# A pool map in plain fp32 from unsplit operands, and the order of the work around it, in a hybrid decoder step on one Trainium2 core

## What is computed

```python
h = modulate(rms_norm(x, g_pre_mix), shift_m, scale_m)
u, q, k, v, z_pool, z_att = jnp.split(h @ w_in, IN_SPLITS, axis=-1)
# branch A, 4 groups of 256 channels, windows 2, 4, 8, 16
pooled = window_mean(u_ext) - u
mixed  = jnp.einsum('btgc,gcd->btgd', pooled, w_map)          # the pool map
y_pool = (mixed * scale) @ w_proj_pool
# branch B: dilated window attention, 3 groups merged by their denominators
y_att  = o @ w_proj_att
mix = (sigmoid(z_pool) * y_pool + sigmoid(z_att) * y_att) @ w_out
x = x + gate_m * rms_norm(mix, g_post_mix)
# then up-projection, causal conv of 3, GeGLU, down-projection, norm
```

## Time and profile before

| | |
|---|---|
| runs, median | 1136.33, 1133.63, 1133.76; 1133.76 us |
| the profiled execution's own time | 1135.69 us |
| its span in the profile | 1133.8 us |
| mean granted TensorE clock | 0.955 |
| PE busy | 1059.3 us (93%), 8653 matmul records |
| DVE / ACT / POOL busy | 485.5 / 417.8 / 119.7 us |
| DMA | 216 MB, mean 191 GB/s |

### The profile page before, as it was taken

How to read it: one execution, slowest core, us unless ns; L and a number is a source line. 1 busy time by engine, 2 the same in 40 slices (tenths; PEclk the granted TensorE clock), 3 DMA queues, 4 the chain that set the end, 5 groups by cost and what they waited for, 6 DMA issues and landing times.

```text
span 1133.8 us, 20595 instructions
## 1 busy us (share of the span) xinstructions
PE 1059.3 (93%) x8653; PEld 991.8 (87%) x8653; DVE 485.5 (43%) x884; ACT 417.8 (37%) x667; POOL 119.7 (11%) x165
## 2 busy tenths in 40 slices
PE   5999999999999999979898795599999999999996
PEld 3899999999999999868748794599999999999994
DVE  5533233322432244254814335656565655522224
ACT  5424423332443234244202233544444544422222
POOL 1000300040004001405402202200000000000000
PEclk8899999999999999979999897699999999999996
DMA  9885767567656774243926537066666666555312
GB/s 324 247 277 199 224 223 250 186 216 244 236 186 212 244 243 131 77 139 120 309 98 199 184 111 252 27 198 225 223 224 222 219 220 210 156 172 162 117 36 75
DMA packets 226856, 216.01 MB, mean 191 GB/s; under 512 B 6173, under 2 KB 191901, under 8 KB 226749
## 3 DMA queue, kind: packets, MB, share of 16 engines
q1 hardware_dynamic: 226765, 214.70, 58.2%
HBM read 207.27 MB, written 96.03 MB: 268 GB/s over the span
## 4 chain that ended last, share of the span: by engine, by line
PE 87%; DVE 5%; ACT 2%; POOL 2%; issue 1%; SPq 1%; DMA 1%; ACTq 0%; POOLq 0%; DVEq 0%
PE acc L1289 74%; PE psT L1581 2%; PE psS L1453 2%; PE psT L1467 2%; PE psS L1333 2%; POOL tha L630 1%; POOL ssq L590 1%; PE psS L1441 1%; PE psS L1343 1%; DMA ada_first<-in_w_ada 1%; PE psT L1481 1%; PE psS L1439 1%; PE psS L1557 1%; DVE xT L1233 1%; ACT norm_u L680 1%
## 5 line engine op out<-in xcount | busy, mean ns | idle before, releaser
L1289 PE MATMUL acc<-act_hi,w_hi 128*128 128x260 f32 x1824 | 379.3, 289 | 20.4 <-DVE act_lo L1138 7.2
L1289 PE MATMUL acc<-act_hi,w_lo 128*128 128x260 f32 x1824 | 371.0, 285 | 0.0
L1289 PE MATMUL acc<-act_lo,w_hi 128*128 128x260 f32 x1824 | 370.7, 285 | 0.0
L892 DVE TENSOR_TENSOR w_lo<-raw,w_hi 128x1024 fp32r<-128x1024 f32 x150 | 191.7, 1279 | 374.7 <-ACT w_hi L651 374.1
L1289 PEld LDWEIGHTS acc<-act_hi,w_hi 128*128 128x128 f32 x1824 | 284.9, 191 | 29.3 <-issue 23.9
L1289 PEld LDWEIGHTS acc<-act_lo,w_hi 128*128 128x128 f32 x1824 | 285.3, 191 | 0.0
L1289 PEld LDWEIGHTS acc<-act_hi,w_lo 128*128 128x128 f32 x1824 | 284.9, 191 | 0.0
L651 ACT ACTIVATE w_hi<-raw 128x1024 fp32r<-128x1024 f32 x150 | 157.0, 1046 | 203.7 <-PE acc L1289 193.7
L1289 PE MATMUL acc<-g_hi,w_hi 128*128 128x260 f32 x352 | 71.0, 283 | 0.0
L1289 PE MATMUL acc<-g_hi,w_lo 128*128 128x260 f32 x352 | 70.8, 282 | 0.0
L1289 PE MATMUL acc<-g_lo,w_hi 128*128 128x260 f32 x352 | 70.6, 282 | 0.0
(11 more groups left out here) (248 smaller groups left out, 1126.9 us busy)
## 6 DMA issues: line engine op xcount, KB each, us to landing
out_k_sample<-in_cache_k_w SPq DMA_DIRECT2D x89, 368.0 KB
out_v_sample<-in_cache_v_w SPq DMA_DIRECT2D x89, 368.0 KB
raw<-in_w_in SPq DMA_DIRECT2D x60, 512.0 KB, 6.1
raw<-in_w_up SPq DMA_DIRECT2D x44, 512.0 KB, 5.8
ada_mid<-in_w_ada SPq DMA_DIRECT2D x11, 1024.0 KB, 9.8
ada_first<-in_w_ada SPq DMA_DIRECT2D x9, 1024.0 KB, 9.4
raw<-in_w_down SPq DMA_DIRECT2D x16, 512.0 KB, 4.1
out_k_sample<-in_cache_k_w SPq DMA_DIRECT2D x16, 511.0 KB
```

The costliest lines, as they stand in the source:

```text
L892: dve.tensor_tensor(w_lo[PLACE[n]][:, 0:cols], raw[:, n % RAW, 0:cols], w_hi[PLACE[n]][:, 0:cols].bitcast(F32), ALU.subtract).then_inc(lo_ ...
L1289: ins_ = pe.matmul(acc[b][:, half, 0:HALF], w, x[:, t, half * HALF:(half + 1) * HALF], start=first and i == 0 and j == 0, stop=last and i ...
```

## The change

The map's sums are made by plain fp32 matmuls straight from `uT` and from `raw` (`map_unit`): two blocks, two halves, no split of either. The map's two units are left out of `PLACE`/`SPLITS`, so the splits that ran for them two units ahead now run for pp0 and pp1. `pooled_hi` and the VectorE half of it go. PE's order is now: map unit 0, then the second fold, move_stat and the transposes, then map unit 1, then spread_shares, then pp0. ScalarE and VectorE follow the same order; `join` comes behind the last sum of the map. The cast rounds move from `MID` places 1 to 6 to places 2 to 7 (round 0 with pp0, round 5 with pp5), the transposes of `u_tail` from the end of the map to the end of pp1. `mixed_hi/lo` are now the memory of `act_hi/lo`, and four of the six places of cached keys and values move to the memory of `qkvT` and `uT`.

```diff
-PLACE = [0, 1, 2] + [n % 2 for n in range(1, len(UNITS) - 2)]
+PLACE = {0: 0, 1: 1, 2: 2}
+for n in range(3, len(UNITS)):
+    if UNITS[n][0] != "map":
+        PLACE[n] = 1 - PLACE[max(m for m in PLACE if PLACE[m] < 2)]
+SPLITS = sorted(PLACE)
+SPLIT = {n: i for i, n in enumerate(SPLITS)}
...
         @block.sync
-                if n >= RAW:
-                    sp.wait_ge(lo_ready, n - RAW + 1)
+                if n >= RAW and n - RAW in SPLIT:
+                    sp.wait_ge(lo_ready, SPLIT[n - RAW] + 1)
+                elif n >= RAW:
+                    sp.wait_ge(unit_done, n - RAW + 1)
...
         @block.scalar
-                            split(N[s] + 2)
+                            split(SPLITS[N[s] + 2])
...
-            weights(PAIRS - 1)
-            pooled_hi(0)
-            pooled_hi(1)
-
-            act.wait_ge(rows_turned, 1)
...
             for pos, (what, m) in enumerate(MID):
-                if 1 <= pos < 7:
-                    i = pos - 1
+                if pos == 1:
+                    weights(PAIRS - 1)
+                    act.wait_ge(rows_turned, 1)
+                    act.activation(qhl[0:64, :], psS[0:64, 0:DA], ACT.Copy)
...
+                if pos == 2:
+                    joined(PAIRS - 1)
+                    act.wait_ge(o_lod, PAIRS)
...
+                if 2 <= pos < 8:
+                    i = pos - 2
...
         @block.tensor
+            def map_unit(m):
+                n = N["map", m, 0]
+                pe.wait_ge(raw_full[n % RAW], 16 * (n // RAW + 1))
+                for q in range(4):
+                    i, g, d = 4 * m + q, 2 * m + q // 2, q % 2
+                    pe.wait_ge(pooled, g + 1)
+                    take(("map", i))
+                    for kt in range(2):
+                        w = blk(raw[:, n % RAW, :], 4 * (q // 2) + 2 * kt + d)
+                        for half in range(2):
+                            ins_ = pe.matmul(acc[SUM["map", i] % 2][:, half, 0:HALF], w, uT[:, 2 * g + kt, half * HALF:(half + 1) * HALF],
+                                             start=kt == 0, stop=kt == 1)
+                    ins_.then_inc(unit_done if q == 3 else part_done, 1)
```

More of the change, by code:

```diff
@@ L451, in load_k @@
                 if i == 2:
-                    done(sp, ("map", 1, 0))
+                    done(sp, ("map", 0, 0))
                 if i >= 4:
@@ L457, in load_v @@
             def load_v(i):
+                if i == 0:
+                    done(sp, ("map", 1, 0))
                 if i >= 2:
@@ L1147, in _ @@
                                                  ALU.mult, ALU.subtract).then_inc(free(("map", i)), 1)
-                    split(N[u] + 2)
+                    if m == 0:
+                        modulation(OADA - 1)
+                        shares(PAIRS - 1)
+                        dve.wait_ge(smp_ready, 1)
+                        dve.tensor_tensor(qhl[32:32 + NG * NB, :], smp_rows[0:NG * NB, :], qhl[0:NG * NB, :].bitcast(F32), ALU.subtract).then_inc(q_split, 1)
+                    else:
+                        join(PAIRS - 1)
                 if what == "pp":
@@ L1592, in _ @@
             for pos, (what, m) in enumerate(MID):
-                slot = ready((what, m, 0))
-                if 1 <= pos < 7:
-                    cast(pos - 1, 0)
-                if what == "map":
-                    for q in range(4):
-                        g, d = 2 * m + q // 2, q % 2
-                        i = 4 * m + q
-                        if pos and q == 2:
-                            cast(pos - 1, 1)
-                        pe.wait_ge(pooled_split, g + 1)
-                        take(("map", i))
-                        ins_ = blocks(("map", i), slot, [(4 * (q // 2) + 2 * kt + d, 2 * g + kt) for kt in range(2)], act_hi, act_lo)
-                        ins_.then_inc(unit_done if q == 3 else part_done, 1)
-                    if m == 1:
-                        pe.wait_ge(pooled, 4)
-                        pe.wait_ge(o_lod, PAIRS)
-                        for k in range(KT):
-                            ins_ = pe.transpose(psT[0:TAIL, k * P:(k + 1) * P], u_tail[:, k, :], ident[:, :])
-                        ins_.then_inc(tail_turned, 1)
+                if what == "map":
+                    map_unit(m)
+                    if m == 0:
+                        fold(OADA - 1)
+                        move_stat(PAIRS - 1)
+                        pe.wait_ge(smpT_ready, PAIRS)
+                        pe.wait_ge(maxed, 2 * PAIRS * STEPS)
+                        for p in range(PAIRS):
+                            ins_ = pe.transpose(psS[0:9 * NB, p * P:(p + 1) * P], smpT[:, p, :, :].rearrange("p a b -> p (a b)"), ident[:, :])
+                        ins_.then_inc(rows_turned, 1)
+                    else:
+                        spread_shares(PAIRS - 1)
+                    continue
+                slot = ready((what, m, 0))
+                if 2 <= pos < 8:
+                    cast(pos - 2, 0)
                 if what == "pp":
@@ L1623, in _ @@
                     blocks(("pp", m), slot, [(i, i) for i in range(KT // 2, KT)], mix_hi, mix_lo, first=False).then_inc(unit_done, 1)
+                    if m == 1:
+                        pe.wait_ge(o_lod, PAIRS)
+                        for k in range(KT):
+                            ins_ = pe.transpose(psT[0:TAIL, k * P:(k + 1) * P], u_tail[:, k, :], ident[:, :])
+                        ins_.then_inc(tail_turned, 1)
                     if m == 6:
```

70 lines of the change are left out of this document (21 added, 49 removed).

## The result

Seven runs of the changed kernel gave a median of 1124.69 us (1123.3 to 1129.85), beside 1134.25 (1133.63 to 1136.33) for seven of the kernel before: a ratio of 0.9917 [0.99, 0.9935], 9.6 us or 0.8% faster. The forecast was 1124.7.

A forecast was written before the change was run, and what follows sets the result against it. PE, with 87% of the last chain, was taken as the bound: 14.8 us earlier at pp1's start, less 3.5 given back, 1.7 for the clock and 0.5 for small waits, net 9.1; 1133.76 - 9.1 = 1124.7 us, range 1121.8 to 1129.0.

The forecast's parts named there:

- The map's matmuls: In the map: 32 plain fp32 matmuls, 64 records at 0.225 us, 14.4 us, 2 us more PE work than before.
- The rival with loads in the open: In the map: weight loads not hidden behind matmuls, up to 7.7 us more, 1132.4 us in all; chance 0.08.
- Emptying the sums: In the map: a buffer is released in 1.7 us, PE makes the next sum in 1.8, so nearly no waits.
- The two new waits: PE waits 1.5 us for `mod` before move_stat and 1.3 us in the middle of pp0 for the cast behind join.
- pp1's start: From the adaLN product's end to pp1: 28.4 us against 43.2 at full clock, so pp1 starts 14.8 us earlier.
- Given back: After pp1's start: u_tail transposes 0.96, casts 1.3 and a longer pp6 wait 1.2, in all 3.5 us lost.
- The loads: At pp2: its load, issued near 504.7 behind o_lod, lands at 508.5, wanted at 508.0; taken to cost nothing.
- The rival's 8 us: At pp2: if its load took 8 us, the second cast's copies come about 2.3 late, 1127.0 us; chance 0.10.
- one fall between the map units: Between the map units: clock at half for 3.4 us after the quiet stretch, costing 1.7 us; chance 0.45.
- a further sign of a fall: Between the map units: transposes do not count as busy for the clock, lengthening the quiet stretch by 0.5 us.
- the rival without a fall: Between the map units: the clock stays up, since idle time is shorter than 1.97 us; 1123.0 us, chance 0.27.
- The slower rival: From the map to pp0: plain fp32 keeps the clock at half, 6.8 us slower than before, 1140.6; chance 0.03.

The follow-up runs named there:

- the fold early: Changed kernel with the second fold behind the map's second sum instead of the fourth, and VectorE's mod behind that sum's mixed_lo: 1123.87 us, ratio 0.9903.
- scores first: Changed kernel with VectorE's split for pp7 moved from before the fifth score sum to behind the softmax's maximum in pp6: 1122.33 us, ratio 0.9893.
- cast late: Changed kernel with the second half of cast round 0 moved from the middle to the end of pp0: 1122.42 us, ratio 0.9889.
- loads early: Changed kernel with SP issuing the loads of pp2 to pp5 before its wait for o_lod and bh: 1126.06 us, ratio 0.9918.
- the two partial kernels: Two kernels, each with one half of the change: plain fp32 map in the old order, 1132.66 us; new order with split operands, 1134.18 us.
- plain fp32 alone: Changed kernel's plain fp32 map, with small steps and spread_shares back ahead of it and casts at places 1 to 6: 1132.66 us, ratio 0.9981.
- the order alone: Kernel before, its splits and fp32r matmuls kept, with small steps and join in the new order and casts one place later: 1134.18 us, ratio 0.9996.

## Why the forecast held, step by step

- **The map's matmuls.** 64 records at 0.225 us, 14.4 us. Measured in the chain of waits, the two units' own rows:

```profile
479.28 7.38 PE acc L1543 x32
...
490.15 7.17 PE acc L1543 x32
```

  14.55 us, 0.227 each. The weight loads behind them are as short as any:

```profile
L1543 PEld LDWEIGHTS acc<-uT,raw 128*128 128x128 f32 x64 | 11.7, 190 | 2.8 <-issue 1.0
```

  190 ns, hidden in a spacing of 227. The rival with loads in the open, 7.7 us, is refuted, and with it the dearer loads that I had drawn from the Trainium skill's rule on fast weight load for non-FP32 inputs ("TensorE: Matmul & The Clock Gate", section "Weight-path perf modes — Fast Weight Load (FWL) and DoubleRow"): if the rule holds, it does not show in the length of these loads, 190 ns now beside 191 for fp32r. The section does not say whether fp32r counts as FP32; if it does, the two kinds of load would be alike by the rule itself, and no run here tells these cases apart.
- **Emptying the sums.** No wait inside either unit, as worked out from 1.7 against 1.8 us. How thin the margin is shows in the run with the fold early: PE came sooner, VectorE still had `shares` and the q split in front, and PE waited 0.50 us at once.
- **The two new waits.** 1.5 and 1.3 forecast, 1.67 and 1.20 measured. The second follows the mechanism of its worked chain: join from 499.27 to 503.49 is 4.2 us (4.1), a copy of 0.61, then the cast. Its terms were less good than its result. The forecast counted two copies, and one was enough; it set 4.4 us of PE's work against the chain, and 3.7 stood there, since the cast that waits cannot cover its own wait; and 4.1 + 1.1 + 0.4 is 5.6, not 5.7. The errors cancel.
- **pp1's start.** 14.8 us earlier at full clock. From the adaLN product's start to pp1's it was 522.79 - 478.55 = 44.24 and is 508.22 - 478.21 = 30.01: 14.2.
- **Given back.** 3.5 forecast. From pp1's start to the cached values it was 51.90 and is 55.26: 3.4. The wait in pp6 went from 3.99 to 5.16 for the reason given, with a split of 2.46 us ending 1.1 us after the product (547.65 + 2.46 = 550.11; 544.40 + 4.62 = 549.02).
- **The loads.** The forecast had pp2 land at 508.5 with ScalarE wanting it at 508.0. It was issued at 504.27, took 5.3 us instead of 3.8, and ScalarE began at 509.60, some 1.3 us after pp0's end had given it the place. I had taken the lateness as nothing, and nothing it was: no wait of PE in pp1 in the profile after, and nothing gained by loading early (stretch 86.23, beside 86.34 for the changed kernel when the clock fell in pp0 too). Where the load took 6.12 us, the cast of 515.30 hung on it by some 0.2 us. The rival's 8 us did not occur: in the five profiles where ScalarE waited for this load it was 5.0 to 6.3 us from the issue to ScalarE's start.
- **The clock, the one term that was off.** I charged 1.7 us for one fall between the map units and 0.5 for small things. In both profiles of the changed kernel the clock stood at 1.00 there, through waits of 1.67 and 1.51 us, and so it did in three more with the same wait (scores first, cast late, loads early). The four transposes, which the forecast took as a further sign of a fall, stood in that place each time. In one of the changed kernel's two profiles the clock fell behind the wait in pp0, which cost 1.5 us. So a fall was priced about right, and put in the wrong place with the wrong chance. The nearest row that I went by, an idle time of 1.97 and then 0.47 us, was a poor guide: with idle times of 1.67 and 1.51 us there was no fall, with 3.74 us there was one. The profiled execution therefore came out as the rival without a fall had it (1123.0; measured 1122.6 of span), while the median came out at the forecast, 1124.69 against 1124.7. That agreement within a tenth is luck: the clock term was some 0.9 us too dear over both profiles (1.7 against 0 and 1.5), and the profiled execution of before, on whose scale I worked, lay 1.4 above the median measured beside the result.
- **The slower rival**, half clock throughout, is refuted by the first window at 1.00 for 29.9 us: plain fp32 at 0.227 us a record keeps the clock up.

The stretches of the two partial kernels, 4.2 and 2.8 us shorter than in the one profile of before, promise more than their medians give (1.5 and 0). For plain fp32 alone that comes out: its profiled execution is its median, but the adaLN product started 1.2 us later in it than before, and the profiled execution of before lay 1.5 above its median (1135.69 against 1134.16). For the order alone the profiled execution was the fastest of ten, 3.9 us below their median, and its mean granted clock, 0.961, the highest; the ten average 0.957. So its other executions spent more time at the lower clock, an estimated 9 us (0.004 x 2 x 1130), worth up to 4.5 us. Where in the kernel they did so no run shows. Nor is it shown what decides whether a wait of 1.2 us brings a fall.

## What to carry to other kernels

When a bound engine meets a chain of small steps of another engine, list for each step what it waits for, and move independent long work between them; but the long work itself must be ready. Here that took both halves at once: the order put the map between the steps, and raw operands made the map ready. Half of the gain up to pp1 was not the waits themselves but the lower clock that had followed them, so here a microsecond of waiting had cost PE about a second one. Measured one by one each half looked worthless (0.2% and nothing, of 0.8%), so a pair of edits that remove each other's reason to wait must be timed as a pair.

After such a move read the waits again: the three that were left in this profile, each a small step queued one place too late, were worth another 6 us for a dozen lines. The step to look at is the one at the head of a list with ready work behind it.

## What the runs showed of the hardware

- Plain fp32 with full 128-column weights runs at the pace of the 64-column ones: 0.227 us a record for 260 columns, beside 0.432 for 512. Two records make one product, so it costs 0.45 us where the three fp32r matmuls cost 3 x 0.129 = 0.39: a sixth more PE time buys the loss of both splits.
- A split on VectorE took 2.46 us beside a product on GpSimd and 1.23 without. It ended 1.09 us behind the product's end (549.02, 550.11), and so it was before (555.24, 556.32): nearly its whole length of 1.23 came after the product, so it did little or nothing while that ran. Two reductions took 4.46 us without and 4.47 where the product ran beside them for the first 1.9 (550.75 to 552.67).
- The granted clock fell to 0.50 for 6.8 us after 3.74 us of idle time and small products (one profile), not at all after 1.67 and 1.51 (five profiles), and for 3.4 us after 1.19 to 1.22 in three of six profiles, one of two of the same code. A fall of 3.4 us cost 1.5 us of dense work. Where it falls is not a property of the code alone.
